# An order of steps of its own for each engine, in the mixers and the seams of a three-block model on one core

## What is computed

```python
# first_block, two layers: mixer 0 is mlstm_mixer, mixer 1 swa_sink_attention
for i in range(DEPTH):
    mix = mlstm_mixer(...) or swa_sink_attention(...)
    x = layer_norm(DEEPNORM_ALPHA * x + mix, mix_ln_g[i], mix_ln_b[i])
    x = layer_norm(DEEPNORM_ALPHA * x + squared_relu_mlp(x, mlp_w_up[i], mlp_w_down[i]), ...)
    x = x + jax.nn.sigmoid(x @ ple_w_gate[i] + ple_b_gate[i]) * (p[i] @ ple_w_proj[i])
# second_block, one layer
h = h + 0.5 * swiglu(rmsnorm(h, ffn1_norm), wg, wu, wd)
h = h + mixed @ w_out        # mixed: nsa_attention (3 kinds of units) and forgetting_attention, each rms-normed
h = h + 0.5 * swiglu(rmsnorm(h, ffn2_norm), ...)
h = h + sigmoid(rmsnorm(h, ple_gate_norm) @ ple_w_gate) * rmsnorm(p @ ple_w_proj, ple_norm)
```

## Time and profile before

| | |
|---|---|
| median of 3 runs | 1200.24 us (1200.07 to 1200.28) |
| profiled execution, span from first to last instruction | 1198.3 us |
| instructions | 16295 |
| PE busy | 1185.0 us (99%) |
| PEld busy | 1009.1 us (84%) |
| DVE busy | 747.1 us (62%) |
| ACT busy | 625.2 us (52%) |
| POOL busy | 42.8 us (4%) |
| DMA | 210.78 MB, mean 176 GB/s |

### The profile page before, as it was taken

One profiled execution on the slowest core, in us unless ns is written; L12 is line 12 of the kernel. 1 busy time (PEld: TensorE's weight loads), 2 busy tenths in 40 slices (PEclk: granted clock), 3 DMA queues, 4 the chain that ended last, 5 costly groups with the idle time before them and its releaser, 6 DMA issues.

```text
span 1198.3 us, 16295 instructions
## 1 busy us (share of the span) xinstructions
PE 1185.0 (99%) x6443; PEld 1009.1 (84%) x6443; DVE 747.1 (62%) x990; ACT 625.2 (52%) x938; POOL 42.8 (4%) x64
## 2 busy tenths in 40 slices
PE   9999999999999999999999999999999999999998
PEld 8887899898777889999888888888878788888887
DVE  6669645556866774554697455447986565554456
ACT  5554544344566544444466434436886674444445
POOL 2000000000000000000001000001111000000000
PEclk9999999999999999999999999999999999999999
DMA  8566555654744355555545565554651336555540
GB/s 290 191 206 209 194 189 165 209 193 159 227 150 141 115 205 199 194 173 198 192 142 188 196 206 180 181 172 144 187 170 71 115 123 211 196 191 172 179 176 36
DMA packets 119963, 210.78 MB, mean 176 GB/s; under 512 B 8320, under 2 KB 67024, under 8 KB 119888
## 3 DMA queue, kind: packets, MB, share of 16 engines
q1 hardware_dynamic: 119344, 209.35, 52.4%
q10 hardware_dynamic: 544, 0.40, 0.1%
HBM read 208.68 MB, written 1.05 MB: 175 GB/s over the span
## 4 chain that ended last, share of the span: by engine, by line
PE 92%; DVE 4%; ACT 2%; issue 1%; POOL 0%; ACTq 0%; DVEq 0%; POOLq 0%
PE psum L341 23%; PE psum L343 23%; PE psum L342 23%; PE psum L349 4%; PE psum L350 4%; PE psum L355 4%; PE psum L1448 2%; PE psum L1435 1%; PE psum L1412 1%; PE psum L853 1%; PE psum L540 1%; DVE wl L324 1%; PE psum L1403 1%; ACT xT_high L831 0%; PE psum L3309 0%
## 5 line engine op out<-in xcount | busy, mean ns | idle before, releaser
L293 DVE TENSOR_TENSOR wl<-ring,wh 128x2048 fp32r<-128x2048 f32 x131 | 300.1, 2292 | 263.3 <-ACT wh L284 263.2
L284 ACT ACTIVATE wh<-ring 128x2048 fp32r<-128x2048 f32 x131 | 250.6, 1915 | 215.0 <-PE psum L343 215.0
L341 PE MATMUL psum<-wh,xT_high 128*128 128x512 f32 (+4 forms) x576 | 225.5, 391 | 0.0
L343 PE MATMUL psum<-wh,xT_low 128*128 128x512 f32 (+4 forms) x576 | 218.9, 380 | 0.0
L342 PE MATMUL psum<-wl,xT_high 128*128 128x512 f32 (+4 forms) x576 | 218.2, 379 | 0.0
L341 PE MATMUL psum<-wh,hidT_high 128*128 128x512 f32 (+2 forms) x472 | 178.7, 380 | 0.2
L342 PE MATMUL psum<-wl,hidT_high 128*128 128x512 f32 (+2 forms) x472 | 178.0, 379 | 0.0
L343 PE MATMUL psum<-wh,hidT_low 128*128 128x512 f32 (+2 forms) x472 | 177.9, 378 | 0.0
L341 PE MATMUL psum<-xT_high,wh 128*128 128x256 f32 x480 | 136.0, 283 | 0.0
L343 PE MATMUL psum<-xT_high,wl 128*128 128x256 f32 x480 | 135.8, 283 | 0.0
L342 PE MATMUL psum<-xT_low,wh 128*128 128x256 f32 x480 | 135.8, 283 | 0.0
(11 more groups left out here) (330 smaller groups left out, 1481.4 us busy)
## 6 DMA issues: line engine op xcount, KB each, us to landing
ring<-in_mlp_w_up SPq DMA_DIRECT2D x32, 1024.0 KB, 5.7
ring<-in_mlp_w_down SPq DMA_DIRECT2D x32, 1024.0 KB, 5.0
ring<-in_ffn_wg SPq DMA_DIRECT2D x44, 512.0 KB, 3.9
ring<-in_ffn_wu SPq DMA_DIRECT2D x44, 512.0 KB, 5.0
ring<-in_ffn_wd SPq DMA_DIRECT2D x22, 1024.0 KB, 5.0
ring<-in_ple_w_gate SPq DMA_DIRECT2D x12, 1024.0 KB, 5.0
ring<-in_w_in SPq DMA_DIRECT2D x10, 1024.0 KB, 5.0
ring<-in_a_w_in SPq DMA_DIRECT2D x8, 1024.0 KB, 10.5
```

What stands on the lines that cost most here:

```text
L284: K.nc.scalar.activation(parts_of(K, n)[0][:, 0:w], K.ring[:, n % SLOTS, 0:w], ACT.Copy).then_inc(K.high_ready, 2)
L293: K.nc.vector.tensor_tensor(low[:, 0:w], K.ring[:, n % SLOTS, 0:w], high[:, 0:w].bitcast(F32), ALU.subtract).then_inc(K.low_ready, 2)
L341: nc.tensor.matmul(out, x[0], w[0], start=start, stop=False)
L343: return nc.tensor.matmul(out, x[1], w[0], start=False, stop=stop)
```

## The change

The `Tail` takes three generators in place of one, and `dve`, `act` and `pe` each walk their own; the three mixers have `pe_steps`, `act_steps`, `dve_steps` (and `nsa_mixer` a `pool_steps`). Each new list holds the steps that its engine acts on, every one of them once, in an order that is no longer that of a common list. What each step does, its waits and its semaphores are as before, and so are SP's list, the feed-forward loops and the last `embed`. The core of the diff (the lists of numbers are cut to one seam):

```diff
-        for step, *args in self.order():
+        for step, *args in self.order[2]():
             if step == "update":
...
-        for step, *args in self.order():
+        for step, *args in self.order[1]():
             if step == "square":
...
-        for step, *args in self.order():
+        for step, *args in self.order[0]():
             if step == "turn":
...
+def after_sinks_pe():
+
+    yield "last", 2, 0
+    yield "last", 3, 0
+    yield "last", 2, 1
     yield "last", 3, 1
+    yield "turn", 0, 0
     yield "turn", 0, 1
     yield "lead", 0
+    yield "lead", 1
+    yield "turn", 1, 0
+    yield "turn", 1, 1
...
     @block.tensor
     def _(pe):
-        for step, *args in steps():
+        for step, *args in pe_steps():
...
-        first_mixer = mlstm_mixer(K, a, layer(after_mlstm, 0, 1, lead=to_ffn))
+        first_mixer = mlstm_mixer(K, a, layer((after_mlstm_pe, after_mlstm_act, after_mlstm_dve), 0, 1, lead=to_ffn))
```

More of the change, by code:

```diff
@@ L981, in after_sinks @@
     yield "high", 0, 1
[L982 to L989, removed]
+    yield "sigmoid", 1
     yield "high", 1, 0
     yield "high", 1, 1
-    yield "low", 1, 0
-    yield "low", 1, 1
[L996 to L1049, removed]
@@ L1052, in after_mlp_1, with after_embed_0_dve @@
[L1052 to L1081, removed]
+def after_embed_0_dve():
+    yield "logit", 0
@@ new lines, in pe_steps @@
+        yield "dense", 1, 0, 1, range(2)
+        yield "dense", 1, 0, 1, range(2, 4)
+        yield "scores", 0
+        yield "scores", 1
+        yield "dense", 1, 1, 1, range(2)
+        yield "turn", 0
+        yield "dense", 1, 1, 1, range(2, 4)
+        yield "scores", 2
+        yield "scores", 3
+        yield "values", 0
+        yield "turn", 1
+        yield "dense", 2, 0, 0, range(2)
+        yield "tiles", 3
+        yield "turn", 2
+        yield "dense", 2, 0, 1, range(2)
+        yield "values", 1
@@ new lines, in pe_steps @@
+        yield "zturn", 0
+        yield "dense", 2, 1, 1, range(2, 4)
+        yield "values", 5
+        yield "values", 6
+        yield "turn", 7
+        yield "out", 0, 0, 0
+        yield "values", 7
+        yield "tiles", 4
+        yield "out", 0, 0, 1
+        yield "zturn", 1
+        yield "scores", 8
+        yield "tiles", 5
+        yield "scores", 9
+        yield "out", 1, 0, 0
+        yield "turn", 8
+        yield "out", 1, 0, 1
+        yield "scores", 10
+        yield "scores", 11
@@ new lines, in pe_steps, with act_steps @@
+        yield "zturn", 2
+        yield "turn", 15
+        yield "values", 14
+        yield "values", 15
+        yield "out", 1, 1, 0
+        yield "given",
+        yield "zturn", 3
+        yield "out", 2, 0, 0
+        yield "last", 3, 0, 0
+        yield "out", 2, 0, 1
+        yield "last", 3, 0, 1
+    def act_steps():
+        yield "high", 2, 0
+        yield "high", 2, 1
+        yield "high", 3, 0
+        yield "high", 3, 1
+        yield "high", 4, 0
+        yield "high", 4, 1
+        yield "tiles", 0
+        yield "tiles", 2
+        yield "tiles", 1
@@ L1784, in steps @@
-        yield "turn", 3
-        yield "mask", 6
-        yield "dense", 2, 0, 1, range(2, 4)
-        yield "values", 2
-        yield "high", 7, 0
-        yield "high", 7, 1
-        yield "low", 6, 0
-        yield "turn", 4
-        yield "scores", 5
-        yield "low", 6, 1
-        yield "dense", 2, 1, 0, range(2)
-        yield "mask", 7
-        yield "group", 0
-        yield "values", 3
+        yield "tiles", 3
+        yield "scores", 3
+        yield "mask", 5
+        yield "sink", 0
@@ L2359, in steps @@
-        yield "low", 13, 1
-        yield "keep", 6
-        yield "hidT", 0
-        yield "turn", 5
-        yield "take", 3, 1
-        yield "hidT", 1
-        yield "keep", 7
-        yield "high", 14, 0
-        yield "high", 14, 1
-        yield "values", 3
-        yield "group", 0
+        yield "dense", 3, 1, 0, range(2)
+        yield "values", 2
+        yield "cw1", 1, 1, range(4, 8)
+        yield "values", 3
+        yield "dense", 3, 1, 1, range(2)
+        yield "scores", 7
+        yield "hidturn", 0
@@ L2385, in steps @@
[L2385 to L2401 removed]
+        yield "values", 9
@@ L2491, in steps @@
-        yield "group", 4
+        yield "turn", 20
+        yield "values", 18
         yield "tiles", 4
+        yield "tiles", 5
+        yield "scores", 23
+        yield "turn", 21
         yield "values", 19
-        yield "turn", 21
-        yield "tiles", 5
-        yield "low", 19, 0
         yield "tiles", 6
         yield "tiles", 7
-        yield "high", 19, 1
-        yield "keep", 22
-        yield "scores", 23
-        yield "keep", 23
+        yield "turn", 22
         yield "values", 20
```

1571 lines of the change are left out of this document (921 added, 650 removed).

## The result

The changed kernel takes **1188.13 us** (median of 4 runs, 1187.99 to 1188.23) beside 1200.26 for the kernel before: the ratio is 0.9898, with a 95% interval of 0.9886 to 0.9909. It is 12.1 us faster. The forecast was 1195.2, 5.0 us faster, with a range of 1191.0 to 1200.0. The runs of the experiments were made later, on four chips; the kernel before took 1200.2 to 1200.3 beside each of them, so differences of 0.1 or 0.2 us to the changed kernel say nothing.

The account below looks back on a forecast made before the run. TensorE was taken as the bound, busy 1185.0 of 1198.3 us, so only its idle time could be won. Terms -1.6 - 0.9 - 0.8 - 0.3 - 1.5 - 0.5 + 0.6 = -5.0 took 1200.24 to 1195.2 us, range 1191.0 to 1200.0.

Parts of the forecast that it names:

- 1 mLSTM mixer and seam: End of mLSTM mixer: reordered lists leave about 0.2 of PE's 1.96 us of waits; -1.6 us, bounds 0 and -2.0.
- 2 seam behind first MLP (with the embedding): Seam behind the first MLP: PE's 0.87 us wait for row tile 1's first half goes; -0.9 us, bounds 0 and -0.9.
- 6 other seams: Second MLP, both embeddings, both gated feed-forwards: squares go behind the high copies; -0.5 us, bounds +0.5 and -1.0.
- 7 new waits: All redone lists, also where PE stood for nothing: new waits cost +0.6 us, bounded by nothing and 4.9.
- the ceiling: Whole kernel: most that can be won, 8.2 us of PE idle time in reach plus 2.4 hidden, about 10.6 us.
- more is hidden in 'busy' than I count: Rival: many more waits under 0.16 us than 15, nearly all removed; 1189.6 us, chance 0.10.
- the three signs of being wrong: PE's idle sum over 11 us, a wait over 1 us where none stood, or a changed loop pace.
- Part 3: Sink mixer: waits before turns 10 and 15, and smaller ones, shrink; -0.8 us, bounds 0 and -1.6.
- Part 4: Sink mixer's seam: second copy hidden, against a third split before the first update; -0.3 us, bounds +1.1 and -1.7.
- Part 5: NSA mixer: 0.7 from named waits and half the small ones, one wait staying; -1.5 us, bounds 0 and -3.8.
- the 1.46 wait: mLSTM mixer: PE's 1.46 us wait for the low half of z^T was to fall below 0.3.
- One of the two 0.69 gaps: Sink seam: of PE's two 0.69 us idle gaps for ACT's copies of turned rows, one was to go.

Follow-up runs that it names:

- e6: Changed kernel with DVE's third split of load parts in the sink seam moved from before the first update to behind the third: 1188.88 us.
- e1: Changed kernel with all nine seams back in the old common order, the three mixers keeping their new lists: 1192.21 us.
- e3: Changed kernel with TensorE back in its old order in eight of nine seams, ACT and DVE keeping their new lists: 1192.23 us.
- e10: Changed kernel with ACT alone back in the common order in the nine seams: 1198.87 us.
- e11: Changed kernel with DVE alone back in the common order in the nine seams: 1194.95 us.
- e5: Changed kernel with ACT's copy of turn 9 in the sink mixer back behind the exponentials of scores 10 and 11: 1189.37 us.
- e13: Changed kernel with one ACT step behind the second MLP, the high half of tile 0's second half, moved behind the embedding's copies: 1190.15 us.
- e4: Changed kernel with ACT and DVE back in the old common order in all nine seams, TensorE keeping its new order: 1201.97 us.
- e8: Changed kernel with PE and ACT in the sink mixer back in the common order, only DVE keeping its new list there: 1195.14 us.
- e2: Changed kernel with the three mixers back in the old common order, all seams new: 1197.09 us.
- e9: Changed kernel with PE in NSA taking tiles 6 and 7 before values 19, ACT copying them before the exponentials of scores 23: 1189.90 us.

## Why the prediction was right in direction and wrong in size

By its parts, with what the table of stretches gives:

| part | predicted | measured |
|---|---|---|
| 1 mLSTM mixer and seam | -1.6 | -2.2 |
| 2 seam behind first MLP (with the embedding) | -0.9 | -1.0 |
| 3 and 4 sink mixer and seam | -1.1 | -4.0 |
| 5 NSA (with its seam) | -1.5 | -3.4 |
| 6 other seams | -0.5 | -1.6 |
| 7 new waits | +0.6 | 0.2 at most |

- **The step that failed is the ceiling**: "only PE's idle time can be won", with 2.4 us added for what "about 15 waits worth the name" hide. For those 15, the gaps over 0.15 us, the sum is right: 7.6 idle, about 10 in cost. What it put at nothing are the 13 smaller gaps (0.7 idle, 2.8 cost) and the places late without any idle time (2.3 to 7.2). Their cost fell by 4 to 6 of the 12.0. The prediction had this as a rival with a chance of 0.10 ("more is hidden in 'busy' than I count") and 1189.6 us; that rival came closest. Its "against", that the matmuls of the seams start 0.23 apart, was read in the dense stretches, where it is true; most of the unseen waits lie between small matmuls and at changes of kind.
- **The gaps themselves were also forecast too low**: the cost of the 15 fell by about 7, where parts 1 to 6 gave 5.6 for everything. PE's idle sum, the sign named for it, came to 7.4 in place of 8 or 9. None of the three signs of being wrong came true, since none looked inside "busy".
- **The range** stopped at 1191.0 "by the bounds of its parts", but those bounds add up to -11.0, or 1189.2. Even that lies above 1188.1.
- **Part 3** was bounded at -1.6 by the same count, and taken at half of it. Part of the 4.0 (1.05 us) needs seam and mixer together, which a sum over parts cannot give.
- **Part 4** charged a third split in front of the first update with up to 1.14. e6 shows that the place in front is the cheap one, by 0.75.
- **Part 5** was right on the wait that stays (0.94, "about 1 us") and, for that reason, gave only half of the small ones. All of their idle time went, and e1 has 3.1 of the 3.4 with the mixer's lists alone.
- **Part 7** had a price and a place but no case for it; the stretches it named show 0.2 us at the most. e3, e10 and e11 show what it would have taken: one list out of step costs 4 to 11 us. That none stands in the new kernel means that the lists were made as a set, and this the walk through one engine at a time could not see.
- What came as predicted: the 1.46 wait gone, the wait behind the first MLP gone (0.9 against 1.0), start and end unchanged within 0.2, the loops' pace of 0.23 unchanged. "One of the two 0.69 gaps" was too low: both went, 0.25 stayed.
- The Trainium skill (Perfetto Trace Analysis, section Identifying the Most-Contended Engine) has matmul busy time as no good measure of how close a kernel is to its limit, and the prediction set that aside. The traces agree: 6.0 us of this busy time went with the same matmuls at the same clock. The share that it names beside it, that of the weight loads, rose from 84 to 85% as the span shrank; it does not tell where a wait stands.

What stays open: the seams' gain is shown to need all three lists, the mixers' only for the sink mixer. How the 3.4 us of NSA and the 2.2 of the mLSTM mixer divide among engines could not be tried. That the places late without idle time are waits is worked out from the pace of equal shapes; it is shown only where a releaser was looked up (the mask in the sink mixer, the low half in e11) and where e5 and e13 put a wait in.

## What to carry to other kernels

On an engine that is 99% busy, measure waits from start to start against the pace of the same shape, not by idle time: here half of the time won had been drawn as "busy", and each wait put in hid 0.2 to 0.3 us there. When the order of one in-order engine is changed, the lists of the others must follow it: one list left behind in the seams cost 4 to 11 us, where all three together brought 4, and it was not the busiest engine that cost most. Before a step is put in front of a wait as cover, look up which buffer it itself waits for.

## What the runs showed of the hardware

TensorE's granted clock fell behind long waits, which I had not expected of waits of 1 to 3 us. In e4, behind a wait of 2.28 us and before one of 2.60, the products run 0.43 apart in place of 0.23, the lower of the two levels (1.2 GHz for 2.4):

```profile
604.37 1.84 PE L355 MATMUL psum<-early_high,xT_low 128*128 128x512 f32 x4 [2.28 <-DVE xT_low L808]
606.01 0.63 PE L341 MATMUL psum<-wh,pT_high 128*128 128x512 f32 x1
606.44 0.63 PE L342 MATMUL psum<-wl,pT_high 128*128 128x512 f32 x1
```

That stretch (590 to 700 us) is 8.9 us longer than in the changed kernel with only 5.0 more idle: about 3.9 are clock and hidden waits. One wait of 1.67 (e13) or 1.72 (e8) left the clock at 1.00; with one of 2.13 in the last seam of e11, before a product at 1169.15, its mean from 1168 to 1173 us is 0.66. Two of e11's 5 runs are at 1193.9 with a mean clock of 1.000, the others at 1195.0 to 1195.7 with 0.998 or 0.999. In e2, with the old NSA mixer's waits of 0.50, 0.34 and 0.96 within 6 us among small matmuls, the profiled execution shows a dip:

```profile
930.00:940.00 10.00, 8.69 (x51) 6.89 (x50) 5.96 (x15) 6.49 (x21) 0.00 (x0) 0.83 0.79 254
```

It does not come every time: 2 of e2's 11 runs have a mean clock of 0.998 and 1198.5 us, the others lie from 1196.9 to 1197.4. The kernel before has it in 3 of 21 runs (1201.6 to 1201.7 with 0.998, against 1200.2). None of the changed kernel's 4 runs does. In e9, with waits of 0.61 and 0.78 before the matmuls at 924.36 and 926.54, the clock has a mean of 0.66 over 5 us:

```profile
925.00:930.00 5.00, 4.22 (x22) 3.36 (x22) 1.68 (x6) 4.82 (x14) 0.00 (x0) 0.66 0.65 223
```

Two of its 4 runs are at 1190.4 and 1190.5, this profiled one among them, and two at 1189.3 and 1189.4 with a mean clock of 1.000. So the clock can fall at a cluster of short waits between small matmuls, in some executions only, and that costs another 1.1 to 1.4 us. Four runs of the changed kernel are too few to say that it never happens there.
